# Feed-forward 1 by seven block products, and the modulation units spread over feed-forward 0 and four down projections

## The reference, cut to what matters

```python
def swiglu(h, w_gate, w_up, w_down):              # 1024 -> 2816 -> 1024
    g = jnp.einsum('bsd,df->bsf', h, w_gate)
    u = jnp.einsum('bsd,df->bsf', h, w_up)
    return jnp.einsum('bsf,fd->bsd', jax.nn.silu(g) * u, w_down)

def rmsnorm(x, g):
    y = xf * lax.rsqrt(jnp.mean(xf * xf, axis=-1, keepdims=True) + EPS)
    return y * g
...
c_act = jax.nn.silu(c)
for l in range(DEPTH):
    mod = c_act @ ada_w[l] + ada_b[l]             # 1024 x 9216, a vector of 9216
    sh1, sc1, g1, sh2, sc2, g2, sh3, sc3, g3 = jnp.split(mod, N_MOD, axis=-1)
```

## Time and profile before

| | |
|---|---|
| runs, median of three | 2996.57 us |
| profiled execution, its own time | 2998.86 us |
| its span | 2997.2 us |
| PE busy | 2951.9 us (98%) |
| DVE busy | 2155.3 us (72%) |
| ACT busy | 1270.2 us (42%) |
| DMA | 357.50 MB, mean 119 GB/s |

### The profile page before, as it was taken

One profiled execution on the slowest core, in us unless ns is written; L12 is line 12 of the kernel. 1 busy time (PEld: TensorE's weight loads), 2 busy tenths in 40 slices (PEclk: granted clock), 3 DMA queues, 4 the chain that ended last, 5 costly groups with the idle time before them and its releaser, 6 DMA issues.

```text
span 2997.2 us, 46288 instructions
## 1 busy us (share of the span) xinstructions
PE 2951.9 (98%) x17262; PEld 2576.8 (86%) x17262; DVE 2155.3 (72%) x3178; ACT 1270.2 (42%) x1903; POOL 189.1 (6%) x267
## 2 busy tenths in 40 slices
PE   8999999999999999999999999999999999999998
PEld 7888888788888889998887899988998878799987
DVE  7577766665777678775788787867775478788753
ACT  4422323465323245452345555425454244654442
POOL 0000001200000000000130000000000023000000
PEclk9999999999999999999999999999999999999999
DMA  4356563413555533343331133442333332123332
GB/s 150 108 188 198 182 205 116 131 43 99 175 181 191 195 106 102 109 141 116 101 91 63 57 106 105 156 153 85 112 106 102 91 99 86 43 92 100 104 107 76
DMA packets 268315, 357.50 MB, mean 119 GB/s; under 512 B 19906, under 2 KB 211764, under 8 KB 268176
## 3 DMA queue, kind: packets, MB, share of 16 engines
q1 hardware_dynamic: 241344, 270.57, 29.2%
q0 software_dynamic: 26352, 84.74, 8.9%
q10 hardware_dynamic: 480, 0.29, 0.0%
HBM read 348.69 MB, written 2.10 MB: 117 GB/s over the span
## 4 chain that ended last, share of the span: by engine, by line
PE 87%; DVE 9%; ACT 2%; issue 2%; DMA 1%; POOL 0%; DVEq 0%; SPq 0%; ACTq 0%
PE bank L2285 18%; PE bank L2287 18%; PE bank L2286 18%; PE bank L2431 9%; PE bank L2434 9%; PE bank L2433 9%; DVE w_lo L1356 1%; PE bank L2308 1%; PE bank L2311 1%; PE bank L2309 1%; DVE h_f L1412 1%; ACT w_hi L774 1%; DVE h_lo L1418 1%; PE bank L2346 1%; DMA swap<-st 0%
## 5 line engine op out<-in xcount | busy, mean ns | idle before, releaser
L1356 DVE TENSOR_TENSOR w_lo<-raw,w_hi 128x1024 fp32r<-128x1024 f32 x328 | 401.1, 1223 | 493.2 <-ACT w_hi L774 489.6
L774 ACT ACTIVATE w_hi<-raw 128x1024 fp32r<-128x1024 f32 x348 | 368.0, 1058 | 850.6 <-PE bank L2287 806.3
L2285 PE MATMUL bank<-h_hi,w_hi 128*128 128x512 f32 x1376 | 541.7, 394 | 5.3 <-DVE w_lo L1356 3.1
L2287 PE MATMUL bank<-h_hi,w_lo 128*128 128x512 f32 x1376 | 536.2, 390 | 0.0
L2286 PE MATMUL bank<-h_lo,w_hi 128*128 128x512 f32 x1376 | 535.7, 389 | 0.0
L2285 PE MATMUL bank<-act_hi,w_hi 128*128 (+1 forms) x1120 | 437.8, 391 | 0.0
L2287 PE MATMUL bank<-act_hi,w_lo 128*128 (+1 forms) x1120 | 436.1, 389 | 0.0
L2286 PE MATMUL bank<-act_lo,w_hi 128*128 (+1 forms) x1120 | 435.8, 389 | 0.0
L2285 PEld LDWEIGHTS bank<-h_hi,w_hi 128*128 128x128 f32 x1376 | 258.4, 188 | 64.4 <-DVE w_lo L1356 5.5
L2287 PEld LDWEIGHTS bank<-h_hi,w_lo 128*128 128x128 f32 x1376 | 258.3, 188 | 54.6
L2286 PEld LDWEIGHTS bank<-h_lo,w_hi 128*128 128x128 f32 x1376 | 258.5, 188 | 51.9
(11 more groups left out here) (379 smaller groups left out, 5655.2 us busy)
## 6 DMA issues: line engine op xcount, KB each, us to landing
raw<-in_ffn_w_in_dram SPq DMA_DIRECT2D x176, 512.0 KB, 3.5
ada_w<-in_ada_w_dram POOLq DMA_DIRECT2D x72, 1024.0 KB, 5.6
raw<-in_ffn_w_out_dram SPq DMA_DIRECT2D x88, 512.0 KB, 3.8
raw<-in_ffn_w_gate_dram SPq DMA_DIRECT2D x44, 512.0 KB, 3.9
raw<-in_ffn_w_up_dram SPq DMA_DIRECT2D x44, 512.0 KB, 3.9
raw<-in_ffn_w_down_dram SPq DMA_DIRECT2D x44, 512.0 KB, 4.2
raw<-in_mix_w_in_dram SPq DMA_DIRECT2D x44, 512.0 KB, 3.7
raw<-in_attn_w_qkv_dram SPq DMA_DIRECT2D x24, 512.0 KB, 3.7
```

The source lines that it names most:

```text
L774: nc.scalar.activation(w_hi[:, nb % SPL, :], raw_slab(nb), ACT.Copy).then_inc(s_hi, 1)
L1356: V.tensor_tensor(w_lo[:, nb % SPL, :], raw_slab(nb), w_hi[:, nb % SPL, :].bitcast(F32), ALU.subtract).then_inc(s_lo, 1)
L2285: T.matmul(dst, wh, mh, start=first, stop=False)
L2287: return T.matmul(dst, wl, mh, start=False, stop=last)
```

## The change

Feed-forward 1 joins the blocked ones, and its norm moves ahead of it. Its ten units go elsewhere: ten units stay in the rounds of feed-forward 0, and the down projections 0 to 3 now hold 8, 8, 2 and 8. A table gives each unit's first step and the slab after which PE does its tiny matmul, always three later; a unit takes DVE's steps `start` and `start + 1`. All down projections with units are written out slab by slab on PE.

```diff
-BLOCKED = (2, 3, 4, 5)
+BLOCKED = (1, 2, 3, 4, 5)
-ADA_GATE_UP = {0: 0, 1: 15}
-ADA_DOWN = {0: range(10, 15), 1: range(25, 30), 2: range(30, 32), 3: range(32, 36)}
+ADA_FIRST = -1
+ADA_DOWN = {}
+_at = 10
+for _f, _starts in ((0, (0, 2, 4, 6, 8, 11, 14, 17)), (1, (1, 3, 5, 7, 10, 12, 14, 17)), (2, (1, 5)), (3, (1, 3, 5, 7, 10, 12, 14, 17))):
+    ADA_DOWN[_f] = [(_at + _n, _s, _s + 3) for _n, _s in enumerate(_starts)]
+    _at += len(_starts)
-        SCALED_AFTER = {0: "n0", 1: "n1", 2: "n2", 3: "n3"}
+        SCALED_AFTER = {0: "n0", 1: "n1", 2: "n2"}
...
             ada_loads(0, ADA_DOWN[1][0][0])
...
+            for f in (1, 2):
+                pool.wait_ge(s_used, N0[f"ffn{f}"] + 74)
+                ada_loads(ADA_DOWN[f][0][0], ADA_DOWN[f + 1][0][0])
...
             def out_phase(name, q_next):                       # ACT
                 nb = N0[name]
+                if q_next not in SCALED_AFTER:
+                    root_table()
                 for j in range(4):
                     split_hi(nb + 2 * j + 2)
...
             def ada_in_down(s):                                # DVE
-                    starts = (0, 4, 8, 11, 15) if len(ADA_DOWN.get(f, ())) > 4 else (0, 4, 11, 15)
...
+                    for u, start, after in ADA_DOWN.get(f, ()):
+                        if s == after:
+                            ada_out(u, bank[0 if after < 11 else 4])
+                    for u, start, after in ADA_DOWN.get(f, ()):
+                        if s == start:
                             ada_half(u, 0)
+                        if s == start + 1:
                             ada_half(u, 1)
                             ada_sum(u, work[:, 3, :])
...
             out_phase("out0", 3, None)                         # DVE, and ACT alike
+            norm_tail(3, "n3", vec[:, r:r + KC], None, N0["ffn1"] + 1)
             ffn(1, 4, None)
...
+                units = ADA_DOWN.get(f, ())                    # PE
+                for n in range(22 if units else 0):
+                    half, kk = n // 11, n % 11
+                    if n == 11:
+                        pe.wait_ge(s_mod, max(u for u, _, after in units if after < 11) + 1)
+                    down(half, kk, signal=kk == 10)
+                    for u, _, after in units:
+                        if after != n:
+                            continue
...
+                        ada_matmul(u, bank[0 if n < 11 else 4])
+                if units:
+                    pe.wait_ge(s_mod, units[-1][0] + 1)
+                    return
...
             out_phase("out0", a1["out_hi"], a1["out_lo"], ...)  # PE
+            mean(3)
             ffn(1, "n3")
```

More of the change, by code:

```diff
@@ L830, in norm_tail @@
                     nc.scalar.activation(sd4[:, 0, :], bank[7][:, 0:NB], ACT.Sqrt, bias=small[:, 65:66]).then_inc(s_sd, 1)
-                if shift is not None and shift % 72 != 24:
+                if hname in KEPT:
                     silu_table()
@@ L866, in blocked_ffn @@
                 n, r, o = N0[f"ffn{f}"], R0[f"ffn{f}"], order(f)
-                shift = {2: 0, 3: 48, 4: 72, 5: 120}[f]
-                l, which = shift // 72, shift % 72 // 48
+                shift = {1: None, 2: 0, 3: 48, 4: 72, 5: 120}[f]
+                l, which = (shift // 72, shift % 72 // 48) if shift is not None else (0, 0)
                 def product_hi(p, j, i):
@@ L1302, in _ @@
             out_phase("out0", 3)
+            norm_tail(3, "n3", None)
             ffn(1, 4)
@@ L1553, in blocked_ffn, with ada_half @@
                 body(1, 4, True)
+            def ada_half(done, half, i=0):
+                dve.wait_ge(s_adaload[half], 16 * (done + 1) + 16 * i)
+                for j in range(4):
+                    k = 4 * half + j
+                    if k:
+                        dve.wait_ge(s_adastep, 8 * done + k + 8 * i)
+                    w = ada_w[:, half, j, :]
+                    if k == 0:
+                        ins = V.tensor_scalar(ada_acc[:], w, cact[:, 0:1], None, ALU.mult)
+                    else:
+                        ins = V.scalar_tensor_tensor(out=ada_acc[:], in0=w, scalar=cact[:, k:k + 1], in1=ada_acc[:],
+                                                     op0=ALU.mult, op1=ALU.add)
+                    ins.then_inc(s_adastep, 1)
@@ L1572, in ada_sum @@
[L1572 to L1585, removed]
@@ L2548, in ffn @@
                     down(half, 9)
-                    if half and len(units) > 2:
-                        pe.wait_ge(s_mod, units[-1] + 1)
                     down(half, 10, signal=True)
```

132 lines of the change are left out of this document (62 added, 70 removed).

## The result

The changed kernel took 3009.71 us (median of 7 runs, 3003.54 to 3011.43), the kernel before 2997.07 in the same session: a ratio of 1.0035, 95% interval 1.0024 to 1.0047. In a second session it was 3011.68 (5 runs) against 2998.94, 1.0042 (1.0028 to 1.0055). So it is slower, by 12.6 us in the medians. The forecast was 2999.5, its range ended at 3005, and "slower" had a chance of 0.26.

A forecast was written before the change was run, and what follows sets the result against it. PE's work plus its waits was taken as the bound, PE being busy 98%. -13.2 + 1.4 + 0.8 + 1.5 + 0.9 + 6.1 + 5.4 = +2.9 us on 2996.57 gave 2999.5 us, range 2991 to 3005.

The forecast's parts named there:

- The rounds and the norm ahead: Feed-forward 1: ten rounds -17.8 us, the part before the second round +4.6, together -13.2; the norm's entry +1.4.
- The table: Root table loaded ahead of the third slab's split, making its low part late for PE: +0.8 us (0 to 1.5).
- Down projection 0: Three more units there cost PE +0.9 us; DVE's work fits and costs nothing more.
- the loads: Rival: loads become the bound in down projection 0, +2 to +4 us, 3001.5 to 3003.5; chance 0.08.
- The waits: Down projections 1 and 3: PE waits 1.1 us before slab 9 and 3.1 before slab 11; stage sums +6.1 and +5.4.
- The third: Down projection 1, steps 12 to 15: DVE's excess work exceeds its lead, so PE waits +1.0 us (0 to 1.5).
- The clock: At feed-forward 1's norm, the lower clock expected after 4.3 us of waiting and one-column matmuls: +1.5 us (0 to 2.7).
- the two long waits: Before slab 11 of down projections 1 and 3, PE waits for a unit's result: +3.1 us each.
- a rival with 0.22: Clock falls after the slab-11 waits in down projections 1 and 3: 3 to 5.6 us more, 3002.5 to 3005.1; chance 0.22.
- The prediction's own sign of being wrong: No idle before slab 11, a granted clock below 1.00 in the down projections, or waits that `ada_w`'s loads end.
- the sum without its clock term: The forecast's sum of +2.9 us for the whole kernel, leaving out the +1.5 for the clock at feed-forward 1's norm.

The follow-up runs named there:

- filled_wait: The changed kernel with 24 filler matmuls between slab 10's unit matmul and the wait before slab 11, in down projections 1 and 3: 3004.39 us.
- spread and filled: The changed kernel with units respaced in down projections 1 to 3 and nine more filler matmuls at feed-forward 1's norm: 2990.33 us.
- early_last: The changed kernel with units respaced, filler at feed-forward 1's norm, root table loaded later, and down projection 0's last unit started in step 16, not 17: 2991.62 us.
- fill_more: The changed kernel with units respaced, root table loaded later, and filler at feed-forward 1's norm, at projection 0's entry and after feed-forward 1: 2992.39 us.

## Why the prediction was wrong, step by step

*The rounds and the norm ahead.* Right. The ten rounds took 201.59 us against 202.43. With the norm, feed-forward 1 gave -12.1 where -13.2 + 1.4 + 1.5 = -10.3 was forecast: 0.8 of the difference is in the rounds, the rest ahead of them.

*The table.* Right: 0.61 us for 0.8.

*Down projection 0.* Its own 122.05 against 121.22 is the +0.8 of three units (0.9), and the loads bound nothing. Missed: its last unit's addition stands in step 20 ahead of the residuals and lengthens the wait at projection 0's entry by 0.43 us.

*The waits.* Right in place, releaser and size: 1.35 for 1.1 and 3.04 for 3.1, in both stages. The third was 1.50 for 1.0, at the end of its stated 0 to 1.5. Units and waits make +6.8 and +5.6 of the two stages, against 6.1 and 5.4. Missed: the 0.76 us for POOL in the second mixer.

*The clock.* Here it failed. The sum's only clock term was 1.5 us at the norm, and that fall came (741.72, 3.4 us). The clock behind the two long waits was put at nothing; that was a rival with 0.22, held back by "3.1 us is short". It measured 1.6 us in each stage: that is what filled_wait gave back there, 3.2 in all. The prediction's own sign of being wrong, a granted clock below 1.00 in the down projections, stands in the windows above: 0.99 in both. The span times the granted clock, meaned over the runs of the second session, is 2983.8 us for the changed kernel and 2982.5 for the one before: +1.3, and the sum without its clock term was +1.4. (That they agree so well is partly luck: feed-forward 1 came out lower than forecast, the waits and projection 0's entry higher, and the second mixer's wait was in no term.) The rest of the span, which is lost to the lower clock, is 25.9 us against 15.1: +10.8 where 1.5 was allowed. (This is a rough split: the clock is given in thousandths, 3 us each in one run, an idle PE loses nothing at half clock, a stretch in a stage that waits for another engine can cost nothing, and slow first products are not in it. For single runs of the kernel before, the product lies anywhere from 2979.2 to 2987.3.) The rival too was priced low: it took the fall as 1.5 to 2.8 us for each wait. One trace shows 1.7 behind each, but filling the two waits brought 7.3 in the medians. So of the 9.7 us that the forecast fell short, 3.2 are shown to be the clock at the two waits, and by the rough split up to 6 are lost to it elsewhere (10.8 less these 3.2 and the 1.5 allowed). Filling the waits brought back some of this as well. How that comes about, when the stretches in unchanged stages shift from trace to trace, stays open.

The Trainium skill (TensorE: Matmul & The Clock Gate, "What's actually happening") has the low clock as the default that activity lifts; the prediction noted that by it a full stop should weigh more than the norms' sums. The traces agree in kind: half clock at the end of each of six full stops of 3.04 us or within 1.4 us of it, full clock after the same time spent in filler.

## What to carry to other kernels

Work that is hidden by its total can still stand in the way by its order: write out the queue of the engine that does it, and look for a result that is asked for one step after the matmul that makes it. Moving one unit's matmul behind the next slab took away 2.5 us of wait and 1.5 us of lost clock, twice. Price a stop of PE with its clock, and get several traces of the kernel before, since one trace may be a lucky one. And where a change bundles a gain with a rearrangement, time each alone: spread and filled, the same idea gave 2990.3 us against 2997.8 for the kernel before.

## What the runs showed of the hardware that I had not expected

The half-clock stretches lasted 3.4 to 10.2 us, at one place differently from trace to trace, and the kernel before had 17.1, 17.1 and 30.7 us of them in three traces while its times were 2998.86, 2999.60 and 2999.89. The third made up 2.0 us of it with its first products, which took 0.40 us each and in the other two 0.63; and the stretches did not all cost half their length: those at feed-forward 3's norm (1697.95) and at 2049.52 cost nothing, as DVE's instructions stand 2.59 us later than in the first trace before the one and 2.60 behind the other. In the third trace they stood at seven places, in the first at three, and two places agree. A wait of 0.44 us followed by 16 one-column sums in 2.92 us lost the clock in two traces of four (one of three of the kernel before, and early_last), and the same sums without any wait in the one trace of fill_more. The waits of 1.35 and 1.50 us between full products never did, a stop of 3.04 us did in six of six.
